# Causal query columns of a hybrid decoder trunk: 512- and 256-column matmuls over two banks per half, and a new order of head 5's mask and the rotary products

## What is computed

```
for l in range(2):
    h = rms_norm(x, attn_norm[l]); proj = h @ w_in[l]            # 1024 -> 3072
    qa, ka, va, qd, kd, vd = split(proj)                         # 8 heads of 64 each
    qa, ka, qd, kd = rope(...)
    out_a = causal softmax attention (one MoBA block of 256 keys = all of them)
    out_d = mixture of three dilated causal windows
    x = x + concat(rms_norm(out_a), rms_norm(out_d)) @ w_out[l]
    x = x + square(relu(rms_norm(x, mlp_norm[l]) @ w_up[l])) @ w_down[l]
return rms_norm(x, final_norm)
```

## Time and profile before

| what | value |
|---|---|
| median of 3 runs | 594.0 us (593.96 to 594.09) |
| the profiled execution | 594.02 us |
| its span, first to last instruction | 592.3 us |
| PE, DVE, ACT, POOL busy | 98%, 67%, 53%, 10% |
| granted TensorE clock, mean | 0.998 |
| DMA | 104.20 MB, mean 176 GB/s |

### The profile page before, as it was taken

The page is one execution under the profiler, slowest core; times in us unless marked ns, Lnnn a source line. Parts: engine busy times, 40 slices in busy tenths (PEclk is TensorE's granted clock), DMA queues, the critical chain, the costliest instruction groups (busy, mean ns, idle before and its releaser), DMA issues.

```text
span 592.3 us, 9370 instructions
## 1 busy us (share of the span) xinstructions
PE 583.1 (98%) x3390; PEld 493.9 (83%) x3390; DVE 398.5 (67%) x645; ACT 312.5 (53%) x528; POOL 60.5 (10%) x67
## 2 busy tenths in 40 slices
PE   8999999999999999999999999999999999999995
PEld 6989877888888888888888888778888888888884
DVE  5875987587756656656379868768775655656634
ACT  5745867475435345344285646774645435335322
POOL 0240330210000000000005124102000000000001
PEclk9999999999999999999999999999999999999999
DMA  8955443348665564564265635441876465564201
GB/s 307 371 183 172 143 143 102 113 147 301 210 231 175 168 241 158 179 246 142 71 205 156 210 113 173 142 143 56 259 252 214 155 230 182 162 235 170 107 0 71
DMA packets 58844, 104.20 MB, mean 176 GB/s; under 512 B 1808, under 2 KB 35136, under 8 KB 58816
## 3 DMA queue, kind: packets, MB, share of 16 engines
q1 hardware_dynamic: 58320, 103.03, 51.8%
q10 hardware_dynamic: 496, 0.81, 0.5%
HBM read 102.79 MB, written 1.05 MB: 175 GB/s over the span
## 4 chain that ended last, share of the span: by engine, by line
PE 94%; issue 2%; POOL 2%; ACT 1%; DVE 1%; POOLq 0%; ACTq 0%; DVEq 0%
PE psum L1188 20%; PE psum L956 17%; PE psum L958 16%; PE psum L957 16%; PE psum L1191 10%; PE psum L977 3%; PE psum L1124 2%; PE psum L1143 2%; PE psum L982 1%; PE psum L1161 1%; PE psum L963 1%; PE psum L946 1%; PE psum L1164 1%; POOL q_t L431 1%; PE psum L1011 1%
## 5 line engine op out<-in xcount | busy, mean ns | idle before, releaser
L670 DVE TENSOR_TENSOR w_lo<-raw,w_hi 128x1024 fp32r<-128x1024 f32 x188 | 226.9, 1239 | 51.3 <-ACT w_hi L500 51.3
L500 ACT CAST w_hi<-raw 128x1024 fp32r<-128x1024 f32 x188 | 186.9, 1048 | 4.6 <-DMA raw<-in_w_in 3.6
L1188 PE MATMUL psum<-xt,w_hi 128*128 128x512 f32 x512 | 160.7, 395 | 0.0
L956 PE MATMUL psum<-w_hi,ot_hi 128*128 128x512 f32 x320 | 127.1, 397 | 0.0
L958 PE MATMUL psum<-w_hi,ot_lo 128*128 128x512 f32 x320 | 124.8, 390 | 0.0
L957 PE MATMUL psum<-w_lo,ot_hi 128*128 128x512 f32 x320 | 124.8, 390 | 0.0
L1191 PEld LDWEIGHTS psum<-xt,w_lo 128*128 128x128 f32 x512 | 96.2, 188 | 22.4
L1191 PE MATMUL psum<-xt,w_lo 128*128 128x256 f32 x512 | 100.7, 278 | 0.0
L1188 PEld LDWEIGHTS psum<-xt,w_hi 128*128 128x128 f32 x512 | 80.2, 189 | 2.4
L614 ACT COPY up_cross<-psum 128x512 f32<-128x512 f32 x32 | 18.8, 587 | 118.8 <-PE psum L1191 118.8
L849 DVE TENSOR_TENSOR up_cross<-psum,up_cross 128x512 f32<-128x512 f32 x32 | 22.1, 690 | 74.2 <-ACT up_cross L614 74.2
(11 more groups left out here) (97 smaller groups left out, 647.0 us busy)
## 6 DMA issues: line engine op xcount, KB each, us to landing
raw<-in_w_up SPq DMA_DIRECT2D x32, 1024.0 KB, 5.6
raw<-in_w_down SPq DMA_DIRECT2D x32, 1024.0 KB, 6.7
raw<-in_w_in SPq DMA_DIRECT2D x21, 1024.0 KB, 5.7
raw<-in_w_out SPq DMA_DIRECT2D x8, 1024.0 KB, 4.8
raw<-in_w_in SPq DMA_DIRECT2D x3, 512.0 KB, 7.8
raw<-in_w_in SPq DMA_DIRECT2D x4, 256.0 KB, 4.7
out<-x SPq DMA_DIRECT2D x3, 256.0 KB, 2.4
raw<-in_w_in ACTq DMA_DIRECT2D x2, 256.0 KB, 5.2
```

What stands on the lines that cost most here:

```text
L500: act.copy(dst, src).then_inc(hi_done, 1)
L670: dve.tensor_tensor(lo_t, src, hi_t, ALU.subtract).then_inc(split_done, 1)
L956: pe.matmul(out, s_hi, m_hi, start=first, stop=False)
L1188: pe.matmul(up_banks[b][:, f, :], w_hi[:, slot, cols[f]], xt[:, k, :, :].rearrange("p a b -> p (a b)"), start=k == 0, stop=False)
```

## The change

Group 3 is projected by `both_tiles`, like group 4: per k one 512-column and one 256-column matmul for each i, in banks 0 and 1 for the first half and 2 and 3 for the second, both layers. So for (3, 0) at s = 28 and (3, 1) at s = 32 ACT copies the cross part and DVE adds it. Heads 4 and 5 take their scores in banks 0 and 1. Head 5's mask, exponential, division and transposes move up a step (mask at s = 30). The rotary products of (3, 0) move from s = 28 to s = 31, those of (3, 1) from s = 32 to s = 33, where they come behind head 6's mask. The split that stood in s = 29 (unit 18) and the rest of attention output 0 and 1 move to s = 30, behind head 5's mask. High parts of units 20 and 21 move from s = 31 and 32 to s = 29 and 30. The waits of PE follow the banks.

```diff
-QK_STEPS = [19, 21, 23, 25, 29, 31, 33, 35, 43, 44, 45, 46, 48, 49, 50, 51]
+QK_STEPS = [19, 21, 23, 25, 29, 30, 33, 35, 43, 44, 45, 46, 48, 49, 50, 51]
+O_LO_AT = {s + int(s == 29): pairs for s, pairs in PV_AT.items()}
-CROSS_AT = [{36: ((4, 0),), 40: ((4, 1),)},
-            {8: ((0, 0), (0, 1)), 13: ((1, 0),), 16: ((1, 1),), 36: ((4, 0),), 40: ((4, 1),)}]
-SUM_AT = [{36: (4, 0), 40: (4, 1)},
-          {8: (0, 0), 9: (0, 1), 14: (1, 0), 16: (1, 1), 36: (4, 0), 40: (4, 1)}]
+LATER_CROSS = {28: ((3, 0),), 32: ((3, 1),), 36: ((4, 0),), 40: ((4, 1),)}
+CROSS_AT = [LATER_CROSS, {8: ((0, 0), (0, 1)), 13: ((1, 0),), 16: ((1, 1),)} | LATER_CROSS]
+LATER_SUMS = {28: (3, 0), 32: (3, 1), 36: (4, 0), 40: (4, 1)}
+SUM_AT = [LATER_SUMS, {8: (0, 0), 9: (0, 1), 14: (1, 0), 16: (1, 1)} | LATER_SUMS]
-ROPE_AT = {10: (0, 0), 12: (0, 1), 14: (1, 0), 18: (1, 1), 28: (3, 0), 32: (3, 1), 37: (4, 0), 41: (4, 1)}
+ROPE_AT = {10: (0, 0), 12: (0, 1), 14: (1, 0), 18: (1, 1), 31: (3, 0), 33: (3, 1), 37: (4, 0), 41: (4, 1)}
-HI_LATE = {28: 3, 30: 2}
-HI_AT = {s + HI_LATE.get(s, int(s % 8 in (0, 4))): s // 2 + HI_AHEAD for s in range(0, 2 * ATT_UNITS, 2)}
+LO_AT = {s + int(s == 29): s // 2 + LO_AHEAD for s in range(1, 2 * ATT_UNITS, 2)}
+HI_AT = {s + int(s % 8 in (0, 4)): s // 2 + HI_AHEAD for s in range(0, 2 * ATT_UNITS, 2)}
...
-            return banks[(1, 2, 4, 5)[h % 4]]
+            return banks[(1, 2, 4, 5)[h % 4] - int(h in (4, 5))]
...
-                if half == 0 and g == 3 and j < 2:
-                    unit_ready(l, 2 * g + j, 1)
-                elif half == 0 and g != 3:
+                if half == 0:
                     unit_ready(l, 2 * g + j // 2, j % 2)
...
                         pe.wait_ge(v_done, l * 4 + half + 1)
+                        pe.wait_ge(masked, l * N_HEADS + half + 1)
+                    elif g == 4 and half == 0:
+                        pe.wait_ge(masked, l * N_HEADS + 6)
                     elif g == 4:
-                        pe.wait_ge(rope_terms, qk_half(l, 3, half) + 1)
-                        pe.wait_ge(masked, l * N_HEADS + 4 + half + 1)
+                        pe.wait_ge(acc_summed, APART[l, 3, 1] + 1)
...
+                if h == 4:
+                    pe.wait_ge(acc_summed, APART[l, 3, 0] + 1)
```

More of the change, by code:

```diff
@@ L732, in rope_products @@
                     dve.wait_ge(*((half_done, half_group(l, g)) if early else (weights_used, used(l, 4 * g + 3))))
[L733 to L736, removed]
+                    raw_qk = qk_banks(g, hg)[:, :, 0:SEQ]
                 a, b = (r[:, hg, :].rearrange("p (i t) -> p i t", i=2) for r in (rope_a, rope_b))
@@ L787, in _ @@
                 for s in range(2 * ATT_UNITS):
-                    u = s // 2 + LO_AHEAD
                     if s == STAT_D + 1:
@@ L811, in _ @@
                         rope_products(l, *ROPE_AT[s])
-                    if s % 2 == 1 and u < 2 * FIRST_UP + 1:
+                    u = LO_AT.get(s, 2 * FIRST_UP + 1)
+                    if u < 2 * FIRST_UP + 1:
                         lo(l, u // 2, u // 2 % RING, u % 2)
-                    if s in PV_AT:
-                        for p in PV_AT[s]:
+                    if s in O_LO_AT:
+                        for p in O_LO_AT[s]:
                             o_to_lo(l, p)
@@ L991, in both_tiles @@
                 return last
[L993 to L997, removed]
             def together(g, k, slot, hg, i):
```

## The result

The changed kernel takes 601.81 us (median of 6 runs, 600.09 to 603.57) against 594.05 (593.89 to 595.76) for the kernel before in the same sessions: ratio 1.0127, interval 1.0115 to 1.0139, slower by 7.8 us where 3.0 were forecast. The profiled execution took 601.84, with a span of 600.1 against 592.3. Most kernels of this study, the one before among them, have now and then an execution some 1.7 us longer, in whose traces (runs 2, 4 and 5) the 256-column matmuls behind 8 us start 0.21 us apart in place of 0.12; medians that mix the two levels are marked "both levels".

What follows compares the result with a forecast made beforehand. PE was taken as the bound, with DVE almost as full over some 10 us per layer. A delay of 1.51 us per layer, PE's gain included, made 2 x 1.51 = 3.0 on 594.02: 597.0 us, range 595.3 to 598.4.

Steps and rivals of the forecast that it cites:

- PE's own gain: Group 3's k rows on PE: 0.70 us in place of 0.717, 0.5 us for two layers, 0.20 before head 4's scores.
- Place of the loss: Head 6's transposes on PE, once per layer, wait 1.3 to 1.9 us for DVE; a small wait at head 5.
- The DVE chain: DVE from head 4's mask at 57.56 to the end of head 6's division at 69.67, where before it ended at 67.55.
- as in 66.60 to 67.55: Head 6's division on DVE, taken at 0.95 us from the earlier trace, with POOL still at work.
- The bound named: High bound: a product of (3, 1) collides with POOL's sums, 0.44 us more, giving 2 x 1.95 and 597.9 us.
- Everything PE does afterwards is 1.51 us later: Head 6's transposes start at about 69.72 in place of 68.21, and PE's later work shifts equally, own gain included.
- the sum of 2 x 1.51: Both layers' delays, 3.0 us, added to the profiled 594.02 to give 597.0 us.
- POOL collides more: Rival: POOL also stretches products of (3, 1) and others, and head 7's division is late: 598.7 us, chance 0.23.
- The rival on the faster side: DVE reaches head 6 in time, leaving only PE's gain: 593.5 to 594.0 us, chance 0.12.
- Later waits: Waits at s = 35, 36, head 7 and group 5 were to be covered by the delay at head 6 itself.

Runs made afterwards that it cites:

- run 2: The kernel before with five extra 128x512 multiplications on DVE ahead of head 6's division in each layer: 603.35 us over both levels, 602.48 and 602.51 at the lower.
- run 4: The changed kernel with the rotary products of (3, 0) back at s = 28: 595.19 us over both levels.
- run 5: The changed kernel with the products of (3, 0) at s = 28 and of (3, 1) at s = 34: 593.93 us over both levels.
- run 5's second form: The kernel of run 5 with head 5's transposes and their copy put back to s = 34: 593.48 us against 593.92 for the kernel before.
- run 1: The changed kernel with 8 matmuls of 512 columns on PE ahead of head 6's wait for its division: 598.61 us.
- run 6: The changed kernel with the split of unit 18 back at s = 29, between the masks of heads 4 and 5: 597.51 us.
- run 7: The changed kernel with POOL's sum of squares 1 and rotary sum of (3, 1) waiting for head 6's division: 597.39 us over both levels, 596.43 and 596.63 at the lower.

## Why the prediction was wrong

It forecast the right mechanism at the right instruction, and left out a second one, the clock, which costs 3.1 of the 7.8 us.

- **PE's own gain**: 0.5 us forecast, 0.44 measured in run 5's second form, and 0.21 before head 4's scores for 0.20. Right.
- **Place of the loss**: head 6's transposes, twice, with head 5's wait for ACT's copy small (0.24) and hidden under it. Right; moving the products of (3, 0) and (3, 1) takes the wait away (run 5).
- **The DVE chain**: 69.67 forecast, 70.40 measured. The terms without POOL hold: masks, the wait of 0.50 for 0.53, outputs, products of (3, 0), sum. Splits 19 and 20 were taken at 1.35 and took 1.13 each (63.71 to 64.84, 67.85 to 68.98), 0.44 less. The products of (3, 1), taken at 1.20, took 1.85, and the division of head 6, taken at 0.95, took 1.42. The step that failed is "as in 66.60 to 67.55": the stretched durations were carried over row by row, but with another order of DVE's work POOL's instructions meet other rows, and DVE's row is the long one only where POOL's had started first. The two rows were 0.65 and 0.47 longer than taken. The bound named (0.44 for one product) was too small for the two together: 597.9 has head 6's transposes at 70.16, and they started at 70.53. PE's wait came to 2.2 us in place of 1.7.
- **"Everything PE does afterwards is 1.51 us later"** and the sum of 2 x 1.51: here the prediction fails outright. It took a wait of PE to cost its own length and counted every matmul behind it at full clock. It cited the full clock of the earlier trace rows as a fact of the kernel, and that fact held for a kernel whose PE had no wait of over 0.4 us but the 1.7 at its very start. The clock's part is 1.52 + 1.61, 3.1 us. With the wait alone the kernel would stand at 598.6 (run 1), 0.2 above the range.
- **Rivals**: "POOL collides more" was the true one of those named. That its 598.7 is what run 1 measures is partly luck: it adds 0.44 for one product and 0.4 for head 7's division; measured were 0.65 and 0.47 more at the products and head 6's division, 0.44 less at the splits, and no delay at head 7. None held the clock, so none reached 601.8. The rival on the faster side needs 1.5 us less on DVE and was rightly given little.
- **Later waits**: none showed at s = 35, 36, head 7 or group 5. Right.

The waits and clocks of all profiles together: behind waits of PE of 0.39, 0.44, 0.70, 0.90 and 1.72 us the clock stayed at 1.00; behind those of 2.19, 2.20 and 2.60 it fell to half for some 3 us. One of the changed kernel's six runs, 600.09 us at a mean clock of 0.994 against 0.991, would fit a fall in only one layer; there is no trace of it. What decides whether a wait is followed by a fall stays open.

## What to carry to other kernels

When PE is gapless, a late producer costs its wait and, when the wait is long enough, also the slow matmuls behind it: price both. Here the waits of up to 1.72 us cost only themselves, and those of 2.19 us and more cost 1.5 to 1.6 us on top. Work moved out of an engine's idle hole into its full stretch costs its full length on the path even if it was free before (with the products of (3, 0) back in the hole, run 4 had a wait of 0.39 in place of 2.19); put it back, or behind the instruction that the bound engine waits for. Between DVE and POOL, don't carry a stretched duration from one row to the same row in a new order; lay both queues side by side and see what now meets what.

## What the runs showed that was not expected

- A scalar multiplication on DVE (`TENSOR_SCALAR` of 128x128 and 128x256) is held by POOL's two-input additions as well as two-input products are: 1.30 against 0.55 us, undone in run 7. The Trainium skill (SBUF — State Buffer, Who interferes with whom) counts `tensor_scalar` among the operations that can take the pair shared with GpSimd, and says that issue order decides who is held. The trace agrees: POOL's sum took 1.64 where DVE's split had started first (67.85 against 68.00), and then DVE's division took 1.42 where the sum's second half ran.
- 0.58 us less in DVE's chain of each layer, 1.2 in all, took 4.3 us off the kernel (run 6), some four times its length, by way of the clock.
